# 64 in place of 48 dense tokens take their u product from gathered rows, with a choice stage of 19 expert groups, and value units stand ahead of the forget gates

## The reference

```python
q = (xt @ w_pq).reshape(T, PEER_HEADS, 2, PEER_HALF)       # 8 heads
s = jnp.einsum('thcd,hcnd->thcn', q, sub_keys)             # 128 keys for each half
s1, i1 = lax.top_k(s[:, :, 0], 16); s2, i2 = lax.top_k(s[:, :, 1], 16)
cand = s1[..., :, None] + s2[..., None, :]                 # top 16 of 256 pairs
idx = i1 * 128 + i2 (of those 16);  g = softmax(top_s)     # 128 experts for each token
h = gelu(einsum('ted,td->te', u[idx], x));  out = einsum('te,ted->td', g * h, v[idx])
```

## Time and profile before

| | us |
|---|---|
| median of 3 runs (lowest, highest) | 3208.12 (3207.56, 3210.55) |
| profiled execution, its own time | 3209.69 |
| its span, first to last instruction | 3208.0 |
| PE busy | 3173.4 (99%) |
| PE weight loads (PEld) busy, beside the matmuls | 2774.8 (86%) |
| DVE busy | 2229.6 (70%) |
| POOL busy | 1232.6 (38%) |
| ACT busy | 1057.9 (33%) |
| moved by DMA | 782.42 MB, mean 244 GB/s |

### The profile page before, as it was taken

How to read it: one execution, slowest core, us unless ns; L and a number is a source line. 1 busy time by engine, 2 the same in 40 slices (tenths; PEclk the granted TensorE clock), 3 DMA queues, 4 the chain that set the end, 5 groups by cost and what they waited for, 6 DMA issues and landing times.

```text
span 3208.0 us, 40186 instructions
## 1 busy us (share of the span) xinstructions
PE 3173.4 (99%) x16351; PEld 2774.8 (86%) x16351; DVE 2229.6 (70%) x2549; ACT 1057.9 (33%) x1053; POOL 1232.6 (38%) x555
## 2 busy tenths in 40 slices
PE   8999999999999999999999999999999999999999
PEld 6877777888878899999998998899899888888887
DVE  5127775222037888777775888888888887888887
ACT  4123333444241233346652322232232233222221
POOL 5443333333434425857864333233223321232222
PEclk9999999999999999999999999999999999999999
DMA  5332222222333248999879899889989997888988
GB/s 206 116 105 89 89 89 86 76 84 110 130 130 126 84 162 305 336 299 297 255 225 315 336 352 361 316 338 361 343 324 350 354 351 287 334 333 338 346 317 300
DMA packets 178550, 782.42 MB, mean 244 GB/s; under 512 B 33008, under 2 KB 83312, under 8 KB 93040
## 3 DMA queue, kind: packets, MB, share of 16 engines
q1 hardware_dynamic: 116224, 461.97, 39.8%
q0 software_dynamic: 62208, 318.86, 27.4%
HBM read 735.30 MB, written 44.40 MB: 243 GB/s over the span
## 4 chain that ended last, share of the span: by engine, by line
PE 91%; DMA 2%; POOL 2%; DVE 2%; issue 1%; ACT 1%; SPq 0%; ACTq 0%; DVEq 0%
PE bank L476 14%; PE bank L478 14%; PE bank L477 14%; PE bank L451 14%; PE bank L453 14%; PE bank L452 14%; PE bank L2128 2%; POOL gate_scratch L882 2%; DMA arena<-in_u_rows,g_idx 1%; PE bank L1947 1%; DVE wl L1222 1%; PE bank L1928 1%; PE bank L2004 1%; DMA gate_scratch<-arena 1%; PE bank L2017 0%
## 5 line engine op out<-in xcount | busy, mean ns | idle before, releaser
L431 ACT ACTIVATE wh<-raw 128x2048 fp32r<-128x2048 f32 x343 | 656.2, 1913 | 1080.6 <-PE bank L478 844.6
L451 PE MATMUL bank<-xh,wh 128*128 128x336 f32 (+1 forms) x2928 | 1002.3, 342 | 10.1 <-DVE wl L1222 10.1
L453 PE MATMUL bank<-xh,wl 128*128 128x336 f32 (+1 forms) x2928 | 990.2, 338 | 0.0
L452 PE MATMUL bank<-xl,wh 128*128 128x336 f32 (+1 forms) x2928 | 988.6, 338 | 0.0
L1222 DVE TENSOR_TENSOR wl<-raw,wh 128x2048 fp32r<-128x2048 f32 x252 | 576.9, 2289 | 213.8 <-ACT wh L431 204.8
L437 POOL TENSOR_TENSOR wl<-raw,wh 128x2048 fp32r<-128x2048 f32 x92 | 424.9, 4618 | 721.2 <-ACT wh L431 721.0
L451 PEld LDWEIGHTS bank<-xh,wh 128*128 128x128 f32 x2928 | 550.9, 188 | 46.1 <-DVE wl L1222 11.0
L452 PEld LDWEIGHTS bank<-xl,wh 128*128 128x128 f32 x2928 | 551.2, 188 | 35.4 <-issue 1.9
L453 PEld LDWEIGHTS bank<-xh,wl 128*128 128x128 f32 x2928 | 550.3, 188 | 35.0
L476 PE MATMUL bank<-wh,xh 128*128 128x512 f32 x1328 | 517.9, 390 | 2.2 <-DVE wl L1222 2.2
L477 PE MATMUL bank<-wl,xh 128*128 128x512 f32 x1328 | 517.2, 389 | 0.0
(11 more groups left out here) (236 smaller groups left out, 2888.2 us busy)
## 6 DMA issues: line engine op xcount, KB each, us to landing
raw<-in_u SPq DMA_DIRECT2D x128, 1024.0 KB
raw<-in_v SPq DMA_DIRECT2D x128, 1024.0 KB
raw<-in_w_in SPq DMA_DIRECT2D x56, 1024.0 KB
arena<-gate_scratch SPq DMA_DIRECT2D x32, 768.0 KB
raw<-in_w_out SPq DMA_DIRECT2D x16, 1024.0 KB
raw<-in_w_pq SPq DMA_DIRECT2D x16, 1024.0 KB
gate_scratch<-arena SPq DMA_DIRECT2D x8, 2048.0 KB
act_scratch<-arena SPq DMA_DIRECT2D x68, 168.0 KB
```

The costliest lines, as they stand in the source:

```text
L431: nc.scalar.activation(wh[s][:], raw[s][:], ACT.Copy).then_inc(hi_done, 1)
L451: nc.tensor.matmul(dst, w_h[:, c], xh[:, c, 0:width], start=(c == 0), stop=False)
L452: nc.tensor.matmul(dst, w_h[:, c], xl[:, c, 0:width], start=False, stop=False)
L453: last = nc.tensor.matmul(dst, w_l[:, c], xh[:, c, 0:width], start=False, stop=(c == KC - 1))
```

## The change

- `PB` is 32: 64 tokens take their u product from gathered rows, u units are 320 columns wide, and there are 64 gathers and dots (32 and 32) in place of 48.
- `LAG` is 19: the choice stage has 76 units, the main stage 13 groups, the tail 76 units. `GATE_FROM` is 42. Slots of the sparse block in the tail: 51 in nine sets (six of 6, three of 5) in place of 40 in eight sets.
- `DOT_UNITS`: the second kind of dot stands in units 36 to 58 (32 dots; two in nine of the 23 units) in place of 37 to 53 (16 dots). Three row buffers serve the first 39. `behind`: one scatter after each of gathers 4 to 40, two after each of 41 to 62, and 47 at the end (before: one or two, then two or three, and 54 at the end).
- Start: x and the weights of the first two value units are loaded in turn, w_f behind them. ACT and DVE split the first value unit's weights after four columns of x. `forget_w` moves from `wh[0]` to `gl`, and `forget_gemm` stands ahead of the fourth value unit, with semaphores of its own.
- Seam to the main stage: DVE does `lo` of units 1 and 2 ahead of `gate_mult(0)`, ACT splits unit 2 ahead of its wait for the gates.

```diff
-LAG = 17
+LAG = 19
-PB = 16
+PB = 32
-GATE_FROM = 34
+GATE_FROM = 42
-LOOK_AT = {0: (8, 9, 10, 11), 1: (14, 18, 22, 26), 3: (59, 60, 61, 62)}
-TURN_AT = (31, 33)
-PAIR_TURN = GATE_FROM + 24
+LOOK_AT = {0: (8, 9, 10, 11), 1: (14, 18, 22, 26), 3: (66, 67, 68, 69)}
+TURN_AT = (39, 41)
+PAIR_TURN = GATE_FROM + 20
...
-             30, 31, 31, 32, 33, 34, 35] + [_k for _k in range(37, 54) if _k != 45]
-PAIR_BUF = [_j % 3 if _j < 30 else _j % 2 for _j in range(PN + NB)]
+             30, 31, 31, 32, 33, 33, 34] + \
+    [36, 36, 37, 38, 38, 39, 40, 40, 41] + sorted([*range(42, 59), 43, 46, 49, 51, 53, 55])
+PAIR_BUF = [_j % 3 if _j < 39 else _j % 2 for _j in range(PN + NB)]
...
-            behind = [0] * 4 + [1 + _j % 2 for _j in range(4, 22)] + [1] * (PN - 22) + [2 + _j % 2 for _j in range(NB - 1)]
+            behind = [0] * 4 + [1] * 37 + [2] * (PN + NB - 42)
...
             for q in range(2):
                 sp.dma_start(acc[:, q, :], x_t[q]).then_inc(xt_loaded[q], 16)
-            load(sp, 1, w_in[0])
+                load(sp, q + 1, w_in[q])
...
+            for q in range(4):
+                for c in range(4 * q, 4 * q + 4):
+                    hi_first(act, c)
+                if q < 2:
+                    split_hi(act, q + 1)
...
             for c in range(KC):
+                if c == 4:
+                    lo(1)
                 lo_first(dve, c)
...
             main_lo(0, 1)
+            main_lo(0, 2)
             gate_mult(0)
...
-                main_lo(g, 2)
+                    main_lo(g, 2)
...
             pe.wait_ge(const_ready, 1)
-            forget_gemm(pe)
-
...
+                    if c == 0:
+                        pe.wait_ge(xl_done, 4 * q + 4)
                     if c == 0 and q == 3:
+                        forget_gemm(pe)
                         spread_rows()
```

89 lines of the change are left out of this document (48 added, 41 removed).

## The result

| | before | after |
|---|---|---|
| median of the runs (lowest, highest), us | 3209.3 (3207.6, 3211.2) | 3256.1 (3249.0, 3260.7) |
| profiled execution, its span | 3209.7, 3208.0 | 3255.6, 3253.8 |
| ratio after to before, 95% interval | | 1.0147 (1.0135 to 1.016) |

The forecast was 3198 us with a range to 3226, so it was wrong in direction and outside its range; the rival on the slower side (3237) fell short too.

The account below looks back on a forecast made before the run. PE was taken as the bound, with DVE, POOL and DMA close behind. Gains of 53.3 us against losses of 43 gave -10.3; 3209.7 less that and 1.6 to the median made 3198 us, range 3174 to 3226.

Parts of the forecast that it names:

- the rival on the slower side: DMA engines bound units 36 to 58 and six tail sets; losses 52 + 6 + 24, 3237 us; chance 0.22.
- Narrower units: All 128 u units: 320 in place of 336 columns saves 6.67 ns in each of 6144 matmuls, 41.0 us.
- Start: Kernel start: PE begins value units 12.7 us earlier, less 7.3 for the forget product and 2.3 for clock; -3.1 us.
- Seam: Start of the main stage: `lo` ahead of the gates removes a 6.9 us stop and 2.3 of slow clock; -9.2.
- Choice stage: 16 more gathers and dots, mostly in units 36 to 58, cost 23 us of lateness and 6 of clock; +29.
- I take 18 for POOL's pace: Units 42 to 58: POOL falls 22 us behind, about 4 of lead absorb the first lateness, so 18 lost.
- the clock: Choice stage: four longer stops of PE each lower its clock, at 1.6 us a stop; 6 us more.
- The DMA term: Gate part of the choice stage: a unit needs 9.7 us of transfers in 8.82; 15 us over 17 units.
- Main stage: Main groups at 60.8 us: DMA share 0.94, DVE busy 55.3, so little lost; +2 us, bounds 0 and 6.
- Tail: Six sets with a sixth slot: late rows stop PE 1.5 to 2 us each, plus 2 for clock; +12 us.
- The sentence on the 358 GB/s: Tail: the skill's HBM limit would make a set 66.7 us, not 65.3, and the sum 3194; not taken as ceiling.
- Weight loads: Rival for the u units: weight loads bind PE, so fewer columns gain nothing; 3221 us, chance 0.03.

Follow-up runs that it names:

- narrow_only: start_seam with u units of 320 in place of 336 columns, the u product of 16 tokens left out; 3191.0 us, ratio 0.9943.
- start_seam: The kernel before with only the new start and new seam (LAG 17, PB 16, dots and scatters as before); 3201.6 us, ratio 0.9982.
- few_scatters: The kernel after with 44 of the 128 scatters left out, those behind gathers 41 to 62; 3219.6 us, ratio 1.0043.
- order2: The kernel after, nothing left out, with DVE's order changed in the main groups and in the tail; 3206.8 us, ratio 0.9997.
- narrow_order: pb16_order with u units of 320 in place of 336 columns, the u product of 16 tokens left out; 3174.3 us, ratio 0.989.
- pb16_order: start_seam with DVE's order changed in main groups and tail, which moves one step in the main groups; 3196.9 us, ratio 0.9968.

## Why the prediction was wrong

The sum missed by 56 us: 20 in the choice stage, 19 in the tail, 10 in the main stage and 7.5 at the seam. The steps that failed are of one kind: I took a lateness of DVE, or at the seam of the gate table, as covered by slack or as paid once (in the main stage by comparing busy sums). The runs showed stops of PE for it, and in the first three of these stages they come again and again.

**Narrower units, -41.0.** The spacing is as forecast (0.147). But "all of it is on the path as long as the others keep up" carried most of the forecast, and whether they keep up at 7.04 us was not looked at: in the order of before the width alone is worth 10.6 us, with the main groups mended 22.6. In narrow_only 14.9 us of it are lost in the main stage, 11.4 in the choice stage (stops of 1 to 4 us) and 9.0 at the seam, where PE comes earlier and the gate table does not.

**Start, -3.1.** Right: 2.8, PE at 13.40 and at half speed until 18.7, the forget product ahead of the fourth unit.

**Seam, -9.2.** 3.3 in start_seam, and 1.7 between the two kernels. The failed step: "the gate table itself, needed four units later (28 us)". It is needed at the third unit, by way of ACT's gelu, and came just then. I had followed who waits for `lo` and not who waits for the gate product.

**Choice stage, +29.** Measured +48.8 (3.0 + 45.8); the bound was 52. Mechanism and place were right for POOL: the sum of 172 us against 150 named the engine that few_scatters convicted, and the stops stand behind dots that wait for rows. The size failed twice. POOL's prices were not off (a scatter 2.19 and a gather 1.86 us in the kernel after, where I had 2.25 and 1.79). The step that failed is "I take 18 for POOL's pace", 22 us of lag less 4 of lead, paid once: each late row holds DVE for up to 9.5 us and PE for 4.3 to 7.0, and it comes six times. Whether a third row buffer there would end this was not tested. And the clock: I counted four stops at 1.6 us; the six stops make 34 us, which leaves about 12 of the gate part's 45.8 for half clock and small stops (an estimate, by subtraction).
The DMA term (9.7 us of transfers in 8.82, 15 us) was wrong: the share fell to 0.85, and with the scatters gone the same gathers fitted (few_scatters, 1444.8 to 1595: share 0.92, PE busy 146 of 150 us).

**Main stage, +2.** Measured +11.9. I compared sums (DVE 55.3 of 60.8, DMA 0.94). What binds is one `lo` behind one dot, nine stops of 1.0 to 2.4 us. Busy shares under 1 don't show that.

**Tail, +12.** Measured +30.6, bound 28. The place (the fourth unit of a set), the number (six) and the cause (the sixth row step bunched ahead of a `lo`, rows late behind it) were right, the size was not: 2.9 to 5.6 us each in place of 1.5 to 2, since the wait for the row (3.69) and the extra `add_row` (2.35) add to a stretch that had 0.5 to spare.
The sentence on the 358 GB/s of the Trainium skill (DMA: Bandwidth & Descriptors, Where 436 GB/s comes from): order2 moved 364 GB/s over 73 us of the tail with PE never waiting. That is not a ceiling here.

**The rivals.** The slower rival had the right side and the wrong cause: not the DMA engines. Its 52 and 24 were nearly the measured 49 and 31; it fell 19 short by the seam's gain, which it left whole (7.5), the main stage (6 for 11.9) and the tail (24 for 30.6), less 3 that it had too much in the choice stage. Weight loads don't bind: 320 columns run at 0.147, and narrow_order's main stage is at its own work of 883.8 us. The share of LDWEIGHTS, which the Trainium skill (Perfetto Trace Analysis, Identifying the Most-Contended Engine) would have us read beside the share of peak FLOPs, did not tell the bound here.

**The chances.** 0.24 for slower was too little. A forecast of 53 us gained against 43 lost rested on the gains being certain and on each loss happening once; the runs showed gains that depend on the same orders as the losses.

## What to carry to other kernels

Shortening the work of the bound engine buys only what the second chain has to spare, and that stands in the order of the other engines, not in their busy shares: for each `lo` read how early it is done, and ask which row step stands ahead of it. Before giving a step more work, try the narrower width with the work left out (one line here); that would have said that 10 of 41 us come through. And when a change loses by order, mend the order before giving it up: the same 64 tokens and 19 groups are at 0.991 of before with two steps of DVE moved and 18 scatters put at the end, 18 us under pb16_order, the 48 tokens and 17 groups with the same steps moved.
